# Long convolution by residues of four: value spectra and inverse over 256 bins, folds on VectorE, five of sixteen product rows on POOL

## The chip, the core and the metric

The kernel runs on one core of a Trainium2 chip. TensorE (PE; its weight loads are listed apart as PEld), VectorE (DVE), ScalarE (ACT), GpSimd (POOL) and SyncE (SP, which here only issues transfers) each run their own list of instructions in order and meet at semaphores. The metric is the device time of one execution of the whole program in microseconds, as a median over runs.

## What is computed

Two layers of a diffusion backbone over 1024 latent tokens and 256 context tokens of width 1024, all in f32. Layer 0 mixes by gated linear attention and by a long convolution over 512 channels; layer 1 by a short convolution; each is followed by a mixture of 32 experts. The change touches only the long convolution of layer 0:

```python
def hyena_filters(L, ...):          # filters h_fwd, h_bwd of length L = 1024, 512 channels each
    ...
    hh = (hh @ w3).reshape(L, 2, HY_WIDTH) * window[:, None]
    return hh[:, 0], hh[:, 1]

def bidir_fftconv(u, h_fwd, h_bwd, skip):
    L = u.shape[1]
    n = 2 * L
    U = jnp.fft.rfft(uf, n=n, axis=1)
    K = jnp.fft.rfft(h_fwd, n=n, axis=0) + jnp.conj(jnp.fft.rfft(h_bwd, n=n, axis=0))
    y = jnp.fft.irfft(U * K[None], n=n, axis=1)[:, :L]
    return y + uf * skip

def hyena_mix(p, filt, conv_w, conv_b, skip):
    x0, x1, v = jnp.split(dwconv3(p, conv_w, conv_b), 3, axis=-1)
    return x0 * bidir_fftconv(v * x1, filt[0], filt[1], skip)
```

## The kernel before, in words

Everything is f32 and lives in one SBUF tensor, `arena`, cut into named pieces by offset; pieces that are dead are given to others, and a semaphore orders the two uses. PSUM has eight banks of 128x512. The spectra are not computed by an FFT but by matmuls with tables of cosines and sines: time is split into even and odd tokens (`par`, 2), the 512 bins into four blocks of 128 (`kt`, 4), and there is a cosine and a sine table (`fn`, 2). The order of all work is the order in which each engine's list is written; there is no scheduler.

The stretch that the change touches runs, per engine, like this.

- **DVE, end of the attention heads.** `hyena_conv` forms `VX` = v * x1, channel block by channel block; the product is L2023 and raises `vx_ready`. The last of four comes at the end of `gla_head(3)`.
- **SP.** After the last projection (`hy_mm`) it loads the filters' hidden layer `HH2` (L593), the filter weights `W3H` (L594) and the 4 MB table `DFT` (L595), in this order. When the filters are windowed (`filt_win`) it loads the 4 MB inverse table `IDFT` (L598). Later it loads two halves of the output projection (L463) and, after the last inverse matmul (`idft_mm`), the 4 MB residual input (L606).
- **PE, `hyena_transposes` (L1379)** turns `VX` to time on partitions; ACT copies it to `VTM` (L976).
- **PE, `spectrum(kt, q)` (L1395).** For each bin block eight spectra of four matmuls 128x512 each, accumulated in one bank: q = 0 to 3 of the values `VTM`, q = 4 to 7 of the filters `HSUM`/`HDIF`. For kt = 0 the four value spectra come first, then the filters are made, then the rest follows.
- **Filters, eight steps t.** PE multiplies `HH2` by `W3H` into two banks (L1412), ACT copies one bank (L987), DVE forms sum and difference (L2041, L2042) and windows the sum (L2046), POOL windows the difference (L702). Between them PE and DVE spread a gate row (L1181, L1895).
- **Products.** ACT copies each spectrum out of PSUM into `UK` (L995), eight pieces of 128x512. There is one `UK`, so the copies of block kt wait until the products of block kt - 1 are done. The spectrum product of a block is four rows of `YF` (real and imaginary parts for even and odd tokens); a row is seven instructions, four products and three sums. DVE makes rows 0 and 2 (L2055, L2058, L2061, L2064), POOL rows 1 and 3 (L713, L717, L720, L725): eight rows each over the four blocks. On DVE, every instruction of a row but the second waits for the one ahead of it (`link`); on POOL each waits (`step`).
- **PE, inverse (L1437).** 4 channel blocks x 2 parities x 2 functions x 4 bin blocks = 64 matmuls 128x512. The first 48 need the products of blocks 0 to 2, the last 16 those of block 3.
- **DVE** adds the skip term and gates (L2073, L2076), `hmix_ready`; then PE starts the output projection (L1474), and DVE adds the residual (L2088, L2089), after the load L606.

## Time and profile before

| | us |
|---|---|
| median of 3 runs | 2678.17 |
| lowest and highest run | 2674.11, 2680.32 |
| the profiled execution | 2692.55 |
| its span (first to last instruction of the profile) | 2690.6 |

The profile is of one execution, which took 14.4 us more than the median. Times inside it are counted from the start of its span. The touched stretch lies between 549 and 751 us of the span. A profile row of the timeline reads: start in us, length in us, engine, line of the kernel, operation, output<-input, shapes, how many instructions were merged, and in square brackets how long the engine was idle before and what released it. One f32 matmul appears as two records on PE and two weight loads on PEld.

### The profile page before, as it was taken

The numbers are of one execution on the slowest core, as the hardware profiler recorded it, in microseconds if no ns is written. First come the engines' busy times: TensorE is split into PE (matmuls) and PEld (weight loads), VectorE is DVE, ScalarE is ACT, GpSimd is POOL, SyncE is SP. The second block draws the span as 40 slices with busy tenths as digits, with TensorE's granted clock in tenths as the row PEclk, the third lists the DMA queues.
The fourth block names the chain that finished last, engine by engine and source line by source line (L and its number), as shares of the span: only waits on it lengthen the run. The fifth ranks groups of instructions, "written<-read, shape, count | busy, mean of one in ns | idle before, by whom it ended". The sixth has DMA issues, their size and how long they took to land. (4 is left out here: it accounts for less than half of the span.)

```text
span 2690.6 us, 33060 instructions
## 1 busy us (share of the span) xinstructions
PE 2498.0 (93%) x14463; PEld 1114.3 (41%) x14464; DVE 1026.4 (38%) x1958; ACT 340.0 (13%) x664; POOL 242.9 (9%) x227
## 2 busy tenths in 40 slices
PE   5999989989999899999999799999999999999991
PEld 3455445544445533333333544444556333333330
DVE  2687477747656422222221411011464222222114
ACT  2211233321011100000000310000111000000001
POOL 2000000017600000000000000000000000000000
PEclk8999999989999899999999899999998999999995
DMA  9475001210120689999998611110006999999975
GB/s 335 173 261 196 16 24 32 77 79 10 63 86 29 255 341 388 381 392 379 371 370 348 222 39 41 30 55 31 24 32 259 355 390 392 398 398 385 382 281 216
DMA packets 121869, 574.15 MB, mean 213 GB/s; under 512 B 11743, under 2 KB 48807, under 8 KB 94712
## 3 DMA queue, kind: packets, MB, share of 16 engines
q1 hardware_dynamic: 104328, 528.56, 51.5%
q0 software_dynamic: 17312, 43.16, 4.1%
q8 instruction: 116, 1.90, 0.3%
q10 hardware_dynamic: 80, 0.26, 0.0%
q14 instruction: 33, 0.27, 0.0%
HBM read 550.71 MB, written 38.01 MB: 219 GB/s over the span
## 5 line engine op out<-in xcount | busy, mean ns | idle before, releaser
L1609 PE MATMUL ps<-arena 128*32 128x512 f32 x6144 | 689.7, 601 | 30.7 <-DMA arena<-in_ex_w_dram 30.3
L1609 PEld LDWEIGHTS ps<-arena 128*32 128x32 f32 x6144 | 199.0, 111 | 453.4 <-issue 452.2
L1633 PE MATMUL ps<-arena 128*32 128x512 f32 x3072 | 343.5, 599 | 12.2 <-DMA arena<-in_ex_w_dram 12.2
L1711 PE MATMUL ps<-arena 128*128 128x512 f32 x768 | 333.3, 596 | 4.5 <-ACT arena L1013 4.5
L2275 DVE TENSOR_SCALAR arena<-ps,gain_x,mod 128x128 f32<-128x128 f32 x384 | 126.8, 402 | 374.4 <-PE ps L1594 374.4
L1474 PE MATMUL ps<-arena 128*128 128x512 f32 x512 | 226.6, 597 | 2.9 <-DVE arena L2076 1.6
L1711 PEld LDWEIGHTS ps<-arena 128*128 128x128 f32 x768 | 146.7, 191 | 188.5 <-issue 188.5
L1633 PEld LDWEIGHTS ps<-arena 128*32 128x32 f32 x3072 | 108.0, 111 | 238.7 <-issue 238.7
L2307 DVE SCALAR_TENSOR_TENSOR arena<-ps,arena,gates 128x512 f32<-128x512 f32 x96 | 72.1, 751 | 268.1 <-PE ps L1633 268.1
L1294 PE MATMUL ps<-arena 128*128 128x512 f32 x384 | 167.3, 593 | 0.7 <-issue 0.7
L2283 DVE TENSOR_TENSOR arena<-arena,ps 128x512 f32<-128x512 f32 x48 | 52.5, 1094 | 273.5 <-PE ps L1609 273.5
L1474 PEld LDWEIGHTS ps<-arena 128*128 128x128 f32 x512 | 95.1, 190 | 113.3 <-issue 109.1
L1073 ACT ACTIVATE arena<-ps 128x512 f32<-128x512 f32 x48 | 28.7, 597 | 745.3 <-PE ps L1576 745.3
L2409 DVE TENSOR_TENSOR arena<-arena,ps 128x1024 f32<-128x1024 f32 x8 | 9.8, 1222 | 284.8 <-PE ps L1711 284.8
L1395 PE MATMUL ps<-arena 128*128 128x512 f32 x256 | 113.6, 607 | 3.8 <-DVE arena L2046 3.1
L744 POOL DMA_INDIRECT expert_rows<-arena x48 | 48.1, 1003 | 754.6 <-DVE arena L2307 754.6
L1294 PEld LDWEIGHTS ps<-arena 128*128 128x128 f32 x384 | 72.0, 190 | 88.1 <-issue 87.6
L1863 DVE SCALAR_TENSOR_TENSOR arena<-arena,silu_c 128x512 f32<-128x512 f32 x120 | 90.2, 752 | 4.3
L734 POOL DMA_INDIRECT arena<-normed_rows,arena x48 | 48.7, 1014 | 377.6 <-PE ps L1594 302.2
L1395 PEld LDWEIGHTS ps<-arena 128*128 128x128 f32 x256 | 49.7, 195 | 66.6 <-issue 61.7
L1071 ACT ACTIVATE arena<-ps 128x512 f32<-128x512 f32 x48 | 28.7, 598 | 355.1 <-PE ps L1609 355.1
L1125 PE MATMUL ps<-constants 128*128 128x256 f32 x270 | 72.1, 419 | 0.0
(276 smaller groups left out, 2193.3 us busy)
## 6 DMA issues: line engine op xcount, KB each, us to landing
arena<-in_ex_w_dram SPq DMA_DIRECT2D x192, 2048.0 KB, 11.9
arena<-in_mod_w_dram SPq DMA_DIRECT2D x24, 2048.0 KB, 8.7
arena<-expert_rows SPq DMA_DIRECT2D x16, 1024.0 KB, 8.1
arena<-in_od_w_in_dram SPq DMA_DIRECT2D x24, 512.0 KB, 6.4
arena<-in_x_dram SPq DMA_DIRECT2D x2, 4096.0 KB, 14.8
normed_rows<-arena POOLq DMA_DIRECT2D x16, 512.0 KB, 2.9
arena<-in_ev_w_in_dram SPq DMA_DIRECT2D x3, 2048.0 KB, 13.1
arena<-in_ev_w_in_dram SPq DMA_DIRECT2D x12, 512.0 KB, 4.2
```

Of the source, the lines that this page charges most:

```text
L734: pool.indirect_dma_start(XG[:, b], None, rows_hn, bass.IndirectOffsetOnAxis(ap=PASS_TOK[:, p:p + 1], axis=0), bounds_check=SEQ - 1, oob_i ...
L1125: nc.tensor.matmul(bank(b)[:, 0:256], ident, cst[:, 0:256], start=True, stop=True)
L1294: ins = nc.tensor.matmul(bank(6 + half), HYP[n % 3][:, j], u_part(half, j), start=j == 0, stop=j == KC - 1)
L1395: ins = nc.tensor.matmul(bank((q + 4) % 8), DFT[:, kt, fn, par, tc * P:(tc + 1) * P], rhs, start=tc == 0, stop=tc == KT - 1)
L1474: ins = nc.tensor.matmul(bank(m % 4), mixed[:, j, i * P:(i + 1) * P], slab(first[half], KC, 512)[:, j], start=j == 0, stop=j == KC - 1)
L1609: ins = nc.tensor.matmul(bank(2 + m)[c:c + n], x[:, j, c:c + n], w_slot(e % 2, m, KC, FE)[:, j], start=j == 0, stop=j == KC - 1)
L1633: ins = nc.tensor.matmul(bank(5 + half)[c:c + n], HT[:, j * P + c:j * P + c + n], w_slot(e % 2, 2, FC, D)[:, j, half * 512:(half + 1) * 51 ...
L1711: ins = nc.tensor.matmul(bank(2 * k + half), slab(L1_IN + c, 3, KC, P)[:, k, j], u_part(half, j), start=j == 0, stop=j == KC - 1)
L1863: link(V.scalar_tensor_tensor(out=acc, in0=w[:, j], scalar=silu_c[:, j, 0:1], in1=acc, op0=ALU.mult, op1=ALU.add))
L2275: ins = V.tensor_scalar(XT[:, b, j * P:(j + 1) * P], bank(j // 4)[:, (j % 4) * P:(j % 4 + 1) * P], gain_x[:, 2 * l + 1, j:j + 1], mod[:, l ...
L2283: return V.tensor_tensor(HS.rearrange("t (c p) -> t p c", p=P), SL.rearrange("t (p c) -> t p c", c=FC), bank(3).rearrange("t (p c) -> t p ...
L2307: V.scalar_tensor_tensor(out=YS[:, b, cs], in0=bank(5 + half), scalar=PASS_GATE[:, p:p + 1], in1=gates[:, 1, cs], op0=ALU.mult, op1=ALU.mu ...
```

## The change

The value sequence is now split by token number modulo four instead of two (`times(par, tc)` gives tokens `par + 2 * (tc // 2) + 4 * ...`). Bins k and 511 - k of a residue differ only in signs and in the swap of cosine and sine, so the spectra of the values are computed for 256 bins, two groups g of 128, and the other 256 follow by sums and differences.

- **`residue(g, i, s)`** replaces the value half of `spectrum`. For each group g and each (function, parity) i it accumulates two matmuls in each of two banks (s = 0, 1): 2 x 4 x 2 x 2 = 32 matmuls 128x512 in place of 64, all ahead of the filters. ACT copies the second bank to `USECOND`, DVE adds and subtracts it from the first bank into `USUM[g]` (16 instructions, semaphore `butterfly`). `USUM[1]` lies over `VTM`, so DVE starts the eight of group 1 when all 16 pairs of matmuls are done. PE starts the filters when six of these eight are done (the second step when all are).
- **`filter_spectrum(kt, q)`**: the 64 filter matmuls as before. They alternate between two sets of four banks, and ACT copies them into `KB`, which has two slots, so block kt waits for the products of kt - 2.
- **Products.** POOL makes rows 1 and 3 of block 0 and row 3 of the others: five rows. DVE makes the other eleven.
- **Folds.** After blocks 1 and 3 DVE folds the two blocks of a group: four sums or differences (`tensor_tensor`) and four `scalar_tensor_tensor` with the scalar -2 or 2, in place in `YF`, 16 instructions in all.
- **Inverse.** For each group, channel block and residue r two matmuls with 256 columns, written to every second column of a bank (`bank(2 * c + r % 2)[:, r // 2::2]`): 64 matmuls of 128x256 in place of 64 of 128x512. Group 0 starts after the first fold, group 1 after the second. `IDFT` is 2 MB in place of 4 MB.
- **Space.** `HH2` now lies over the buffer that DVE reads as x1 for the last `VX`. SP therefore waits for the last `vx_ready` before it loads `HH2`; `W3H` and `DFT` stand behind it in SP's list.

PE's list from the last transposes to the end of the inverse, before (L1379 transposes, L1395 spectra, L1412 filters, L1181 gate row, L1437 inverse):

```order
L1379 MATMUL ps<-constants,arena 128x128 x8
L1395 MATMUL ps<-arena 128x512 x16
L1412 MATMUL ps<-arena 128x512 x4
L1181 MATMUL ps<-constants,mod 128x64 x8
...
L1395 MATMUL ps<-arena 128x512 x112
L1437 MATMUL ps<-arena 128x512 x64
```

and now (L1420 residues, L1451 filters, L1430 filter spectra, L1474 inverse):

```order
L1403 MATMUL ps<-constants,arena 128x128 x8
L1420 MATMUL ps<-arena 128x512 x32
L1451 MATMUL ps<-arena 128x512 x4
L1205 MATMUL ps<-constants,mod 128x64 x8
...
L1430 MATMUL ps<-arena 128x512 x64
L1474 MATMUL ps<-arena 128x256 x64
```

Sixteen more matmuls stand ahead of the filters, 48 fewer behind them, and the inverse has the same count at half the columns.

SP's list around the table load, before:

```order
L593 DMA arena<-filter_hidden 64x1024 [waits flt_in,hy_mm]
L594 DMA arena<-in_hy_w_dram 64x1024
L595 DMA arena<-in_dft_dram 128x8192
L598 DMA arena<-in_idft_dram 128x8192 [waits filt_win]
```

and now:

```order
L617 DMA arena<-filter_hidden 64x1024 [waits vx_ready,flt_in,hy_mm]
L618 DMA arena<-in_hy_w_dram 64x1024
L619 DMA arena<-in_dft_dram 128x8192
L622 DMA arena<-in_idft_dram 128x4096 [waits filt_win]
```

The wait for `vx_ready` is new, and `DFT` is behind it.

DVE's list at the end of block 1, now (L2105 ends a product row, L2115 and L2118 are the fold, L2099 and L2102 begin the next block's first row); before, the next block's row followed at once:

```order
L2105 TENSOR_TENSOR arena<-arena 128x512 [waits dve_step]
L2115 TENSOR_TENSOR arena<-arena 128x512 [waits yf_pool,yf_dve]
L2115 TENSOR_TENSOR arena<-arena 128x512 x3
L2118 SCALAR_TENSOR_TENSOR arena<-arena 128x512 [waits butterfly] x4
L2099 TENSOR_TENSOR arena<-arena 128x512 [waits uk_ready,butterfly]
L2102 TENSOR_TENSOR arena<-arena 128x512
L2108 TENSOR_TENSOR arena<-arena 128x512 [waits dve_step]
```

Eight instructions of DVE have come in between two blocks, and again behind the last.

```diff
--- before.py
+++ after.py
@@ -91,18 +91,18 @@
+    low = np.arange(HALF // 2).reshape(2, P)
+    k = np.stack([low[0], HALF - 1 - low[0], low[1], HALF - 1 - low[1]]).reshape(HALF)
@@ -192,11 +192,33 @@
-        IDFT = at(38912, 2, 2, KT * HALF)
+        IDFT = at(38912, 2, 2, SEQ)
...
-        UK = at(0, 8, HW)
+        USUM = [at(0, 8, HW), at(34816, 8, HW)]
+        USECOND = at(30720, 4, HW)
+        KB = at(43008, 2, 4, HW)
+        POOL_ROWS = ((1, 3), (3,), (3,), (3,))
+        DVE_ROWS = [[r for r in range(4) if r not in rows] for rows in POOL_ROWS]
+        def rows_before(rows, kt):
+            return sum(len(r) for r in rows[:kt])
+        def times(par, tc):
+            first = par + 2 * (tc // 2) + 4 * (tc % 2) * P
+            return slice(first, first + 4 * P - 3, 4)
+        def product_terms(kt, row):
+            ua, ub, uc, ud = [USUM[kt // 2][:, 4 * (kt % 2) + q] for q in range(4)]
+            ka, kb, kc, kd = [KB[:, kt % 2, q] for q in range(4)]
+            return (((ua, ka), (ub, kb), (uc, kc), (ud, kd)),
+                    ((ua, kb), (ub, ka), (uc, kd), (ud, kc)),
+                    ((ua, kc), (ub, kd), (uc, ka), (ud, kb)),
+                    ((ua, kd), (ub, kc), (uc, kb), (ud, ka)))[row], ((1, -1, -1), (1, 1, 1))[row // 2]
+        def quarter(g, r, fn):
+            return YF[:, 2 * g + r // 2, (2 * fn + r % 2) if r < 3 else 3 - 2 * fn]
...
-        HH2_EARLY, HH2, W3H = at(47104, SEQ), at(2304, SEQ), at(21504, SEQ)
+        HH2_EARLY, HH2, W3H = at(47104, SEQ), at(20480, SEQ), at(21504, SEQ)
@@ -590,17 +613,18 @@
+            sp.wait_ge(vx_ready, HC)
@@ -704,26 +728,24 @@
-                pool.wait_ge(uk_ready, 8 * (kt + 1))
...
+                pool.wait_ge(butterfly, 8 * (kt // 2 + 1))
+                pool.wait_ge(uk_ready, 8 + 4 * (kt + 1))
...
+                for done, row_ in enumerate(POOL_ROWS[kt]):
+                    terms, signs = product_terms(kt, row_)
@@ -977,22 +999,24 @@
-            for q in range(4):
-                act.wait_ge(dft_mm, q + 1)
-                nc.scalar.activation(UK[:, q], bank((q + 4) % 8), ACT.Copy).then_inc(uk_ready, 1)
+            for g in range(2):
+                for i in range(4):
+                    act.wait_ge(dft_mm, 8 * g + 2 * i + 2)
+                    if g:
+                        act.wait_ge(butterfly, 2 * (i + 1))
+                    nc.scalar.activation(USECOND[:, i], bank((2 * i + 4) % 8 + 1), ACT.Copy).then_inc(uk_ready, 1)
...
-                if kt:
-                    act.wait_ge(yf_dve, 2 * kt)
-                    act.wait_ge(yf_pool, 2 * kt)
-                for q in range(0 if kt else 4, 8):
-                    act.wait_ge(dft_mm, 8 * kt + q + 1)
-                    nc.scalar.activation(UK[:, q], bank((q + 4) % 8), ACT.Copy).then_inc(uk_ready, 1)
+                if kt >= 2:
+                    act.wait_ge(yf_dve, rows_before(DVE_ROWS, kt - 1))
+                    act.wait_ge(yf_pool, rows_before(POOL_ROWS, kt - 1))
+                for q in range(4):
+                    act.wait_ge(dft_mm, 16 + 4 * kt + q + 1)
+                    nc.scalar.activation(KB[:, kt % 2, q], bank(4 * (kt % 2) + q), ACT.Copy).then_inc(uk_ready, 1)
@@ -1377,7 +1401,7 @@
-                                                  VX[:, c, par + 2 * tc * P:par + 2 * (tc + 1) * P - 1:2], ident)
+                                                  VX[:, c, times(par, tc)], ident)
@@ -1385,36 +1409,51 @@
-            def spectrum(kt, q):
-                fn, par = (q % 4) // 2, q % 2
-                if kt:
-                    pe.wait_ge(uk_ready, 8 * (kt - 1) + q + 1)
+            def residue(g, i, s):
+                fn, par = i % 2, i // 2
+                if g:
+                    pe.wait_ge(butterfly, 2 * (i + 1))
+                elif i == 2:
+                    pe.wait_ge(omix_ready, 2 * HEADS)
+                for tc in (2 * s, 2 * s + 1):
+                    ins = nc.tensor.matmul(bank((2 * i + 4) % 8 + s), DFT[:, 2 * g, fn, par, tc * P:(tc + 1) * P], VTM[:, par, tc],
+                                           start=tc == 2 * s, stop=tc == 2 * s + 1)
+                ins.then_inc(dft_mm, 1)
+            def filter_spectrum(kt, q):
+                fn, par = q // 2, q % 2
+                if kt >= 2:
+                    pe.wait_ge(uk_ready, 8 + 4 * (kt - 2) + q + 1)
...
-                    rhs = VTM[:, par, tc] if q < 4 else (HSUM, HDIF)[fn][:, par * KT + tc]
-                    ins = nc.tensor.matmul(bank((q + 4) % 8), DFT[:, kt, fn, par, tc * P:(tc + 1) * P], rhs,
-                                           start=tc == 0, stop=tc == KT - 1)
+                    ins = nc.tensor.matmul(bank(4 * (kt % 2) + q), DFT[:, kt, fn, par, tc * P:(tc + 1) * P],
+                                           (HSUM, HDIF)[fn][:, par * KT + tc], start=tc == 0, stop=tc == KT - 1)
...
-                for q in range(4):
-                    spectrum(0, q)
+                for g in range(2):
+                    for i in range(4):
+                        for s in range(2):
+                            residue(g, i, s)
...
+                    else:
+                        pe.wait_ge(butterfly, 14 + 2 * t)
...
-                                         HH2[0:HID, par + 2 * tc * P:par + 2 * (tc + 1) * P - 1:2],
+                                         HH2[0:HID, times(par, tc)],
...
-                            pe.wait_ge(uk_ready, 4)
+                            pe.wait_ge(butterfly, 16)
@@ -1422,38 +1461,32 @@
-                    for q in range(8):
-                        if kt == 1 and q == 0:
-                            pe.wait_ge(mod_gate, 4)
-                        if kt or q >= 4:
-                            spectrum(kt, q)
+                    if kt == 1:
+                        pe.wait_ge(mod_gate, 4)
+                    for q in range(4):
+                        filter_spectrum(kt, q)
...
-                def part(c, par, kts, first, last):
+                def part(c, r, g):
...
-                        for kt in kts:
-                            ins = nc.tensor.matmul(
-                                bank(2 * (c % 4) + par), YF[:, kt, 2 * fn + par, c * P:(c + 1) * P],
-                                IDFT[:, fn, par, kt * HALF:(kt + 1) * HALF],
-                                start=first and fn == 0 and kt == kts[0], stop=last and fn == 1 and kt == kts[-1])
+                        ins = nc.tensor.matmul(
+                            bank(2 * c + r % 2)[:, r // 2::2], quarter(g, r, fn)[:, c * P:(c + 1) * P],
+                            IDFT[:, g, fn, r * 256:(r + 1) * 256],
+                            start=g == 0 and r < 2 and fn == 0, stop=g == 1 and r >= 2 and fn == 1)
...
-                pe.wait_ge(yf_dve, 2 * (KT - 1))
-                pe.wait_ge(yf_pool, 2 * (KT - 1))
-                for c in range(HC):
-                    for par in range(2):
-                        q = (2 * c + par + 4) % 8
-                        pe.wait_ge(uk_ready, 8 * (KT - 1) + q + 1)
-                        part(c, par, list(range(KT - 1)), True, False)
-                pe.wait_ge(yf_dve, 2 * KT)
-                pe.wait_ge(yf_pool, 2 * KT)
-                for c in range(HC):
-                    for par in range(2):
-                        part(c, par, [KT - 1], False, True).then_inc(idft_mm, 1)
+                for g in range(2):
+                    pe.wait_ge(butterfly, 16 + 8 * (g + 1))
+                    for c in range(HC):
+                        for par in range(2):
+                            if g == 0:
+                                pe.wait_ge(uk_ready, 16 + 2 * c + par + 1)
+                            part(c, par, g)
+                            ins = part(c, par + 2, g)
+                            if g:
+                                ins.then_inc(idft_mm, 1)
@@ -2032,6 +2065,17 @@
+            for g in range(2):
+                u = USUM[g]
+                for i, (plus, minus, turned) in enumerate(((0, 4, 0), (2, 6, 1), (1, 7, 0), (3, 5, 0))):
+                    dve.wait_ge(dft_mm, 16 if g else 2 * (i + 1))
+                    dve.wait_ge(uk_ready, 4 * g + i + 1)
+                    first, second = bank((2 * i + 4) % 8), USECOND[:, i]
+                    V.tensor_tensor(u[:, plus], first, second, ALU.add).then_inc(butterfly, 1)
+                    if turned:
+                        first, second = second, first
+                    V.tensor_tensor(u[:, minus], first, second, ALU.subtract).then_inc(butterfly, 1)
@@ -2047,11 +2091,11 @@
-                dve.wait_ge(uk_ready, 8 * (kt + 1))
...
+                dve.wait_ge(butterfly, 8 * (kt // 2 + 1))
+                dve.wait_ge(uk_ready, 8 + 4 * (kt + 1))
...
+                for done, row_ in enumerate(DVE_ROWS[kt]):
+                    terms, signs = product_terms(kt, row_)
@@ -2059,9 +2103,20 @@
+                if kt % 2:
+                    g = kt // 2
+                    dve.wait_ge(yf_pool, rows_before(POOL_ROWS, kt + 1))
+                    y, z = YF[:, kt - 1], YF[:, kt]
+                    folds = ((y[:, 0], z[:, 0], 1), (y[:, 2], z[:, 2], -1), (y[:, 1], z[:, 3], 1), (y[:, 3], z[:, 1], 1))
+                    for p, q, sign in folds:
+                        V.tensor_tensor(p, p, q, ALU.add if sign > 0 else ALU.subtract).then_inc(butterfly, 1)
+                    for n, (p, q, sign) in enumerate(folds):
+                        dve.wait_ge(butterfly, 16 + 8 * g + n + 1)
+                        V.scalar_tensor_tensor(out=q, in0=q, scalar=-2.0 * sign, in1=p, op0=ALU.mult, op1=ALU.add)\
+                            .then_inc(butterfly, 1)
```

## Rows read from the trace of the kernel before

**Rows 1.** The page, first part: busy time of each engine, share, instructions.

```profile
PE 2498.0 (93%) x14463; PEld 1114.3 (41%) x14464; DVE 1026.4 (38%) x1958; ACT 340.0 (13%) x664; POOL 242.9 (9%) x227
```

**Rows 2.** Busy time by stretch: start:end, length, each engine, granted clock, DMA share, GB/s.

```profile
core 0: us, PE busy (x) PEld busy (x) DVE busy (x) ACT busy (x) POOL busy (x), PEclk, DMA share, GB/s
552.27:567.60 15.33, 15.33 (x32) 6.58 (x32) 0.00 (x0) 1.79 (x3) 0.00 (x0) 0.91 0.00 0
567.60:595.90 28.30, 24.28 (x97) 14.71 (x96) 24.51 (x28) 5.37 (x9) 10.62 (x8) 0.88 0.00 1
595.90:612.36 16.46, 16.46 (x34) 7.25 (x35) 0.55 (x2) 2.39 (x4) 0.00 (x0) 0.89 0.63 256
612.36:636.00 23.64, 23.64 (x57) 10.46 (x56) 22.05 (x14) 0.01 (x1) 22.49 (x14) 1.00 0.00 0
636.00:718.20 82.20, 82.03 (x192) 36.20 (x191) 66.18 (x42) 12.07 (x24) 66.48 (x42) 1.00 0.08 26
718.20:749.45 31.25, 31.23 (x73) 13.49 (x71) 10.08 (x14) 0.00 (x0) 1.04 (x1) 1.00 0.20 68
```

**Rows 3.** Timeline and DMA list (KB each, us to landing): the tables and the first spectra.

```profile
528.51 0.49 SPq L593 DMA_DIRECT2D arena<-filter_hidden  x1
529.69 0.58 SPq L595 DMA_DIRECT2D arena<-in_dft_dram  x1
...
arena<-in_dft_dram SPq DMA_DIRECT2D x1, 4096.0 KB, 14.6
arena<-in_idft_dram SPq DMA_DIRECT2D x1, 4096.0 KB, 12.6
...
548.32 1.22 DVE L2023 TENSOR_TENSOR arena<-arena 128x1024 f32<-128x1024 f32 x1
...
552.27 15.42 PE L1395 MATMUL ps<-arena 128*128 128x512 f32 x32 [0.69 <-ACT arena L976]
```

**Rows 4.** Timeline: DVE in a filter step, and PE's restart behind the filters.

```profile
570.33 0.69 DVE L2041 TENSOR_TENSOR arena<-ps,arena 128x512 f32<-128x512 f32 x1 [19.46 <-issue]
570.93 0.68 DVE L2042 TENSOR_TENSOR arena<-ps,arena 128x512 f32<-128x512 f32 x1
...
595.90 4.63 PE L1395 MATMUL ps<-arena 128*128 128x512 f32 x6 [3.08 <-DVE arena L2046]
```

**Rows 5.** Timeline: products on DVE and POOL, and ACT's copies behind them.

```profile
612.36 0.69 DVE L2055 TENSOR_TENSOR arena<-arena 128x512 f32<-128x512 f32 x1 [15.91 <-ACT arena L995]
...
614.25 1.59 POOL L717 TENSOR_TENSOR arena<-arena 128x512 f32<-128x512 f32 x1
...
614.75 1.64 DVE L2064 TENSOR_TENSOR arena<-arena 128x512 f32<-128x512 f32 x1
...
616.43 1.64 DVE L2058 TENSOR_TENSOR arena<-arena 128x512 f32<-128x512 f32 x1
...
635.99 4.03 ACT L995 ACTIVATE arena<-ps 128x512 f32<-128x512 f32 x8 [23.67 <-POOL arena L720]
...
640.13 0.69 DVE L2055 TENSOR_TENSOR arena<-arena 128x512 f32<-128x512 f32 x1 [5.34 <-ACT arena L995]
```

**Rows 6.** Timeline: DVE and POOL instructions of 512 columns with the other engine silent.

```profile
549.46 1.40 DVE L2000 SCALAR_TENSOR_TENSOR arena<-ps,cols,arena 128x512 f32<-128x512 f32 x2
...
577.40 1.26 POOL L702 TENSOR_TENSOR arena<-arena 128x512 f32<-128x512 f32 x1 [2.42 <-DVE arena L2042]
...
762.46 0.69 DVE L2088 TENSOR_TENSOR arena<-ps,gates 128x512 f32<-128x512 f32 x1 [11.52 <-DMA arena<-in_x_dram]
763.19 0.69 DVE L2089 TENSOR_TENSOR arena<-arena 128x512 f32<-128x512 f32 x1
```

**Rows 7.** Timeline: matmuls of 256 columns, of 64 spread columns, and the inverse.

```profile
220.93 3.70 PE L1257 MATMUL ps<-arena 128*128 128x256 f32 x16
...
571.25 2.00 PE L1181 MATMUL ps<-constants,mod 128*128 128x64 f32 x16
...
694.26 55.17 PE L1437 MATMUL ps<-arena 128*128 128x512 f32 x128 [0.17 <-ACT arena L995]
```

More of the change, by code:

```diff
@@ L329, in build @@
         uk_ready = sem("uk_ready")
+        butterfly = sem("butterfly")
         yf_dve = sem("yf_dve")
@@ L705, in _ @@
             for kt in range(KT):
-                pool.wait_ge(uk_ready, 8 * (kt + 1))
-                ua, ub, uc, ud, ka, kb, kc, kd = [UK[:, q] for q in range(8)]
+                pool.wait_ge(butterfly, 8 * (kt // 2 + 1))
+                pool.wait_ge(uk_ready, 8 + 4 * (kt + 1))
                 t0, t1 = CTMP[:, 2], CTMP[:, 3]
-                for row_, terms, signs in ((1, ((ua, kb), (ub, ka), (uc, kd), (ud, kc)), (1, -1, -1)),
-                                           (3, ((ua, kd), (ub, kc), (uc, kb), (ud, ka)), (1, 1, 1))):
+                for done, row_ in enumerate(POOL_ROWS[kt]):
+                    terms, signs = product_terms(kt, row_)
                     base += 1
@@ L717, in _ @@
                         step(nc.gpsimd.tensor_tensor(t1, x, y, ALU.mult), base)
-                        dst = YF[:, kt, row_] if q == 2 else t0
+                        op = ALU.add if signs[q] > 0 else ALU.subtract
                         if q == 2:
-                            nc.gpsimd.tensor_tensor(
-                                dst, t0, t1, ALU.add if signs[q] > 0 else ALU.subtract).then_inc(yf_pool, 1)
-                            pool.wait_ge(yf_pool, 2 * kt + row_ // 2 + 1)
+                            nc.gpsimd.tensor_tensor(YF[:, kt, row_], t0, t1, op).then_inc(yf_pool, 1)
+                            pool.wait_ge(yf_pool, rows_before(POOL_ROWS, kt) + done + 1)
                         else:
                             base += 1
-                            step(nc.gpsimd.tensor_tensor(
-                                dst, t0, t1, ALU.add if signs[q] > 0 else ALU.subtract), base)
+                            step(nc.gpsimd.tensor_tensor(t0, t0, t1, op), base)
             def gather(l, p):
@@ L2049, in _ @@
             for kt in range(KT):
-                dve.wait_ge(uk_ready, 8 * (kt + 1))
-                ua, ub, uc, ud, ka, kb, kc, kd = [UK[:, q] for q in range(8)]
+                dve.wait_ge(butterfly, 8 * (kt // 2 + 1))
+                dve.wait_ge(uk_ready, 8 + 4 * (kt + 1))
                 t0, t1 = CTMP[:, 0], CTMP[:, 1]
-                for row_, terms, signs in ((0, ((ua, ka), (ub, kb), (uc, kc), (ud, kd)), (1, -1, -1)),
-                                           (2, ((ua, kc), (ub, kd), (uc, ka), (ud, kb)), (1, 1, 1))):
+                for done, row_ in enumerate(DVE_ROWS[kt]):
+                    terms, signs = product_terms(kt, row_)
                     step(V.tensor_tensor(t0, terms[0][0], terms[0][1], ALU.mult))
```

18 lines of the change are left out of this document (8 added, 10 removed).

## Prediction

> **What bounds the kernel now.** I read the page's first part, then busy time by stretch, then the timeline of each engine across the touched part. PE is busy 93% of the span and DVE 38% [rows 1], so less work on PE looks like a gain; the question is whether PE ends last in this stretch and still would. By stretch [rows 2]: from 552.27 the 16 value matmuls of block 0 (15.33 us), from 567.60 the filters (28.30, in which PE, ACT and DVE hand each step on in turn), from 595.90 the filter matmuls of block 0 until the first product (16.46), then 105.84 us from 612.36 to 718.20 in which PE is full (82.03 of 82.20) and DVE and POOL nearly so (66.18 and 66.48 of 82.20; 22.05 and 22.49 of 23.64 in block 0). Last, 31.25 us of inverse alone. Two things stand close together here: PE, and the pair DVE with POOL. An engine at 66 of 82 is no cover for much more work.
>
> Why DVE and POOL are so full: a DVE product lasts 0.69 us at the start of a block and 1.64 while POOL works, with starts 1.68 apart (614.75, 616.43), and POOL's lasts 1.59 [rows 5]. With the other silent, DVE starts the next linked instruction after 0.73 us (762.46, 763.19) and POOL needs 1.26 [rows 6]. Each POOL instruction thus costs DVE 1.68 - 0.73 = 0.95 us; they do not run side by side.
>
> That agrees with the Trainium skill, "SBUF — State Buffer", section "Who interferes with whom": a DVE instruction with two SBUF inputs and a GpSimd one that reads SBUF exclude each other for the whole instruction. By that rule, taken with whole durations, my sum below would be 2697.5; the trace agrees with the exclusion, not with its full length, and I go by the row.
>
> **The change step by step**, in times of the profiled execution.
>
> (a) The table. SP issued L593 at 528.51 and `DFT` 1.18 later, which landed 14.6 after its issue; the last `vx_ready` comes at 548.32 + 1.22 = 549.54 [rows 3]. Now SP waits for it with `HH2`, and `W3H` and `DFT` are queued behind. `DFT` is there at 549.54 + 1.18 + 14.6 = 565.3, and PE, which started at 552.27, waits for it: **+13.0**. The other 4 MB table landed in 12.6 [rows 3]: bound +11.0. Nothing hides this; PE's next work all needs the table. The strided transposes lie in this wait and cost nothing.
>
> (b) 16 more value matmuls ahead of the filters. 64 matmuls took 55.17 us, 0.86 each [rows 7]: **+13.8**. Their butterflies and copies for group 0 run beside PE (DVE idle 19.46 us there, [rows 4]), and banks are free a group later.
>
> (c) The eight butterflies of group 1 start only after the last matmul, and the filters wait for six. Unlinked instructions on DVE start 0.60 apart (570.33, 570.93) [rows 4]: 3.6, and 0.2 for the semaphores: **+3.8**.
>
> (d) PE then restarts after a pause. What that costs is seen at 595.90, after 3.08 us idle [rows 4]: the stretch took 16.46 at a mean granted clock of 0.89 [rows 2], so partly at the lower level of 1.2 GHz, where 16 matmuls are 13.8, one ACT copy 0.5 (4.03 / 8, [rows 5]) and semaphores 0.2. So 1.9 are lost, and as the first filter steps pass through PE in turn: **+1.9** (bounds 0 and 1.9).
>
> Filter matmuls then start 13.0 + 13.8 + 3.8 + 1.9 = 32.5 later, at 628.4, and the first product (16.46 unchanged) at 644.9. The 48 value matmuls that are gone behind this point were PE's; PE now needs 64 x 0.86 = 55 us for the filters and is done at about 685, long before the products.
>
> (e) DVE. Eleven rows of seven; alone a row is 0.60 + 6 x 0.73 = 5.0: 55.0. The folds: four unlinked at 0.60 and four `scalar_tensor_tensor` at 0.70 (two in 1.40, [rows 6]), 5.2, twice: 10.4. POOL's five rows are 35 instructions, all of them while DVE is busy: 35 x 0.95 = 33.3. Together **98.7** against 105.84: **-7.1**, end at 743.6. The gaps of about 4 to 5 us between blocks (5.34, [rows 5]) go, since `KB` has two slots: block 2's copies run while block 1 is multiplied. POOL pauses before block 3 until DVE ends block 1, which moves its instructions but not their number. Bounds: linked instructions at 0.60 in the 36 places where DVE is alone, -4.7; pairs as long as the two lone durations together, 1.26 + 0.69 = 1.95, +9.5. I take 1.68, since the rows show it with the same two kinds of instruction.
>
> (f) Inverse. Group 0 starts near 705 and is hidden behind the products. Group 1, 32 matmuls of 256 columns, stands bare: 16 records of 256 columns took 3.70 with the last one's tail [rows 7], so half of 0.86 holds, 13.8; PE has been idle some 20 us, so the restart again, 1.9: **15.7** against 31.25: **-15.6**. Writing to every second column is not in the trace; nearest are 16 records of 64 columns to every eighth in 2.00, 0.125 each [rows 7], which shows no penalty but could hide a doubling: bounds 0 and +13.8. I take 0.
>
> (g) Hidden: the second half of the output weights is issued at about 738 and, half of a 14.6 us table, is there by 753 for a use near 766. `IDFT` is half as long and 80 us early. The residual load L606 follows the last inverse matmul as before, and DVE waits for it as before (11.52, [rows 6]), so the end moves with the inverse.
>
> **Sum**: 32.5 - 7.1 - 15.6 = **+9.8**. The profiled execution would go from 2692.55 to 2702.4; on the median, 2678.17, this is **2688.0**. PE loses 32 + 32 matmuls' worth (55 us) and the path gains none of it: behind the filters 22.7 are won, ahead of them 32.5 are lost.
>
> **Rivals.**
>
> *Slow inverse.* The half-wide matmuls do not run at half the time. The Trainium skill ("TensorE: Matmul & The Clock Gate", section "The mechanism") says that a weight load overlaps with matmuls in flight only when they sit in different row groups, which full 128-row matmuls never do. A load is 36.20 / 191 = 0.19 us [rows 2]; laid bare in group 1, 64 x 0.19 = 12.2: **2700.2**. Against it: 16 records of 256 columns with 16 such loads in 3.70, where bare loads would make 6.5 [rows 7]. Doubled writes would give +13.8: 2701.8. Together 0.08.
>
> *Small prices all low.* DVE starts linked instructions 0.60 apart (-4.7) and PE restarts at no cost (-3.8): +1.3, **2679.5**, no difference. For it: both are bounds read off rows; against it, the pairs with a link at 0.73 [rows 6] and the 0.89 clock [rows 2]. 0.12.
>
> *Faster.* DVE and POOL stop excluding each other, because their operands now lie elsewhere in `arena` (`USUM`, `KB` in place of one `UK`). DVE then takes 0.73 throughout, 33.3 less, while POOL alone needs 35 x 1.26 = 44 and does not bind: 9.8 - 33.3 = -23.5, **2654.7**. It breaks even at a pair of 1.68 - 9.8 / 35 = 1.40 us and is faster by more than 0.2% below 1.24. Against it: 1.64 and 1.59 in every block, whatever the operands (66.18 and 66.48 us for 42 instructions each, [rows 2]). 0.04.
>
> **How the numbers follow.** Forecast 0.76, between about +4 (table in 12.6, one restart free, part of the link bound) and +19 (pairs at 1.95): 2682 to 2697.5. The range takes in most of the no-difference rival too: 2678 to 2698. What a measurement of this kernel can tell from no change is about 0.2%, 5.4 us. Slower: 0.73 of the forecast and the slow inverse, 0.81. Same: 0.03 and 0.11, 0.14. Faster: 0.05.
>
> **What the profile after would show.** (a) PE's first value matmul at 565, released by the DMA of `DFT`, not by ACT. (b, c) last value matmul near 594, first filter matmul 4 us later, released by DVE. (e) DVE without a gap from 645 to 743, with 1.64 us instructions as long as POOL runs and 0.69 behind it; POOL with one pause of some 7 us. (f) PE idle from about 685 to 705 and 721 to 743, then 32 matmuls in 15.7. The prediction is wrong if the table lands with PE not waiting, if DVE's pairs are not 1.68, or if the last 32 matmuls take over 20 us.

## The result and the profile after

| | before | after |
|---|---|---|
| median, us | 2678.17 (5 runs) | 2701.21 (5 runs) |
| lowest and highest | 2671.59, 2680.32 | 2695.31, 2706.11 |
| span of the profiled execution | 2690.6 | 2704.1 |

The ratio is 1.0077, with a 95% interval of 1.0059 to 1.0095: the change makes the kernel slower by 23.0 us on the medians. The direction was as forecast; the forecast was +9.8.

The page of the changed kernel begins so (busy time, share of the span, instructions; [rows 1] answers to it):

```profile
span 2704.1 us, 32967 instructions
PE 2466.2 (91%) x14399; PEld 1116.0 (41%) x14400; DVE 1045.4 (39%) x2011; ACT 336.7 (12%) x656; POOL 208.5 (8%) x206
```

PE is busy for 31.8 us less than in [rows 1], and the whole takes longer. Busy time by stretch, with the boundaries at the steps of the prediction, answers to [rows 2]:

```profile
core 0: us, PE busy (x) PEld busy (x) DVE busy (x) ACT busy (x) POOL busy (x), PEclk, DMA share, GB/s
562.38:592.30 29.92, 29.92 (x64) 12.93 (x64) 5.15 (x8) 4.18 (x7) 0.00 (x0) 0.92 0.00 1
596.19:638.33 42.14, 41.85 (x96) 24.05 (x97) 26.20 (x30) 4.78 (x8) 10.60 (x8) 0.52 0.00 0
638.33:654.87 16.54, 16.54 (x35) 7.31 (x36) 0.55 (x1) 2.39 (x4) 0.00 (x0) 0.89 0.36 128
654.87:753.54 98.67, 56.76 (x159) 31.39 (x157) 96.36 (x93) 6.62 (x12) 55.75 (x35) 0.82 0.10 34
753.54:769.90 16.36, 16.29 (x64) 13.68 (x64) 10.11 (x15) 0.00 (x0) 0.00 (x0) 0.86 0.13 50
```

The second row is the surprise. It is the filters, and PE has the same matmuls in it as before (96 records, 97 in [rows 2]), but is busy for 41.85 us of 42.14 where it was busy for 24.28 of 28.30, at a mean granted clock of 0.52: the lower level, 1.2 GHz, for nearly the whole stretch. The other rows are close to what was forecast. The timeline of PE (start, length, line, operation; in brackets the idle time before and what ended it):

```profile
562.38 29.95 PE L1420 MATMUL ps<-arena 128*128 128x512 f32 x64 [12.77 <-DMA arena<-in_dft_dram]
596.19 6.00 PE L1451 MATMUL ps<-arena 64*128 64x512 f32 x8 [3.87 <-DVE arena L2077]
602.12 3.67 PE L1205 MATMUL ps<-constants,mod 128*128 128x64 f32 x16
605.73 7.21 PE L1451 MATMUL ps<-arena 64*128 64x512 f32 x8
...
638.33 57.00 PE L1430 MATMUL ps<-arena 128*128 128x512 f32 x128 [0.29 <-DVE arena L2090]
...
753.54 16.29 PE L1474 MATMUL ps<-arena 128*128 128x256 f32 x64 [21.31 <-DVE arena L2118]
```

The wait for the table, the wait for the butterflies and the inverse of 256 columns are all where they were expected. What was not: a pair of filter steps (four matmuls with 64 rows of weights, eight records) takes 7.21 us, and a gate row 3.67. In the timeline of the kernel before, the same lists take 3.71 and, as in [rows 7], 2.00:

```profile
573.18 3.71 PE L1412 MATMUL ps<-arena 64*128 64x512 f32 x8
```

By steps, each from the end of the last `VX` product (549.54 before, 547.58 after) to the end of the inverse:

| step | before | after | measured | forecast |
|---|---|---|---|---|
| (a) `VX` to first value matmul | 2.73 | 14.80 | +12.1 | +13.0 |
| (b) value matmuls | 15.33 | 29.94 | +14.6 | +13.8 |
| (c) pause for butterflies | 0 | 3.87 | +3.9 | +3.8 |
| (d) filters | 28.30 | 42.14 | **+13.8** | +1.9 |
| until the first product | 16.46 | 16.54 | +0.1 | 0 |
| (e) products and folds | 105.84 | 98.67 | -7.2 | -7.1 |
| (f) inverse, bare part | 31.23 | 16.29 | -14.9 | -15.6 |
| sum | 199.89 | 222.25 | **+22.4** | +9.8 |

The sum agrees with the medians (+23.0), and 11.9 of the 12.6 us that the forecast lacks are step (d). The two spans differ by 13.5 us only, since everything outside these steps took 8.9 us less in the profile after. What stands behind the inverse took between 1919 and 1941 us in the profiles of this case (1941.2 before, 1934.3 after). I take that for the scatter of single executions, and from here on the kernels are compared over the stretch from the start of the last transposes to the end of the inverse: 199.8 us before, 222.2 after.

### The profile page after: what moved, and what is told of

Its sections match the earlier page's. It is cut to its first block and busy times, and to the rows that moved or that the text cites. A ratio compares the mean times of both kernels' runs of the same rounds, so it can differ in the third digit from the quotient of the medians.

```text
span 2704.1 us, 32967 instructions
## 1 busy us (share of the span) xinstructions
PE 2466.2 (91%) x14399; PEld 1116.0 (41%) x14400; DVE 1045.4 (39%) x2011; ACT 336.7 (12%) x656; POOL 208.5 (8%) x206
## 5 line engine op out<-in xcount | busy, mean ns | idle before, releaser
L1744 PE MATMUL ps<-arena 128*128 128x512 f32 x768 | 334.9, 599 | 4.5 <-ACT arena L1037 3.1
L1507 PE MATMUL ps<-arena 128*128 128x512 f32 x512 | 226.6, 597 | 2.9 <-DVE arena L2131 1.6
L1744 PEld LDWEIGHTS ps<-arena 128*128 128x128 f32 x768 | 147.7, 193 | 189.1 <-issue 189.1
L1318 PE MATMUL ps<-arena 128*128 128x512 f32 x384 | 167.3, 594 | 0.7 <-issue 0.7
L1507 PEld LDWEIGHTS ps<-arena 128*128 128x128 f32 x512 | 95.4, 191 | 112.6 <-issue 108.8
L1318 PEld LDWEIGHTS ps<-arena 128*128 128x128 f32 x384 | 72.2, 191 | 87.9 <-issue 87.4
L1242 PE MATMUL ps<-arena 128*128 128x512 f32 x160 | 71.2, 602 | 0.0
L1474 PE MATMUL ps<-arena 128*128 128x256 f32 x128 | 32.6, 423 | 41.9 <-DVE arena L2118 21.3
```

Source lines behind the costliest of these rows:

```text
L1242: ins = nc.tensor.matmul(bank((2, 3, 6)[i % 3]), u_cols(i, j), w[:, j], start=j == 0, stop=j == KC - 1)
L1318: ins = nc.tensor.matmul(bank(6 + half), HYP[n % 3][:, j], u_part(half, j), start=j == 0, stop=j == KC - 1)
L1507: ins = nc.tensor.matmul(bank(m % 4), mixed[:, j, i * P:(i + 1) * P], slab(first[half], KC, 512)[:, j], start=j == 0, stop=j == KC - 1)
L1744: ins = nc.tensor.matmul(bank(2 * k + half), slab(L1_IN + c, 3, KC, P)[:, k, j], u_part(half, j), start=j == 0, stop=j == KC - 1)
```

## Experiments on the filters: why the clock was low

My theory after the result: PE stands still for 3.87 us, its clock drops to the lower level, and the filter matmuls with their gate rows do not bring it back, so that PE runs 42 us of work at 1.2 GHz. The first two windows of the filters show where it fell:

```profile
596.19:602.12 5.93, 5.93 (x8) 2.46 (x8) 3.03 (x5) 0.60 (x1) 1.15 (x1) 0.62 0.00 0
602.12:605.70 3.58, 3.58 (x17) 3.49 (x16) 2.71 (x3) 0.60 (x1) 1.88 (x2) 0.50 0.01 2
```

A mean of 0.62 over 5.93 us is about 1.4 us at the full level and the rest at half (an estimate from this row): here the clock fell only when PE was at work again. In the execution with the table first, below, the first pair takes 7.18 us and is slow from its start. The pause comes before the fall in both. Rivals: the 12.77 us wait for the table ahead of the values did it, or the new way of reading `HH2` (tokens modulo four, a stride of four in the weights) makes these matmuls slow.

**The pause filled.** Nine matmuls of 256 columns with the identity, whose result nobody reads, run while DVE makes the butterflies:

```diff
                             residue(g, i, s)
+                pe.wait_ge(uk_ready, 5)
+                spare(9, 5)
                 pe.wait_ge(flt_in, 96)
```

> The changed kernel with nine idle matmuls of 256 columns (into a bank that nobody reads any more) between the last value matmul and the filters, so that PE does not stand still while DVE forms the eight butterflies of group 1; they are work on no result. Theory (clock): the pause of 3.87 us is what put PE to 1.2 GHz for the whole filter stretch, so the stretch from the first filter matmul to the first filter spectrum goes from 42.1 us back to about 28.5, and the time falls by about 13.6 us against the changed kernel, to a ratio near 1.003 of the kernel before. Rival (stride): the filters are slower since HH2 is read at every fourth token instead of every second; then the stretch stays at 42 us and the ratio at 1.008. Rival (long wait): the 12.8 us wait for the table is what the clock does not recover from; then it also stays at 42.

Measured: ratio 1.0019 (0.9999 to 1.0039), stretch 208.7, that is 13.5 less than the changed kernel. PE's timeline and the window of the filters:

```profile
592.61 4.05 PE L1149 MATMUL ps<-constants 128*128 128x256 f32 x18
596.64 3.79 PE L1453 MATMUL ps<-arena 64*128 64x512 f32 x8
600.36 2.00 PE L1205 MATMUL ps<-constants,mod 128*128 128x64 f32 x16
596.64:625.03 28.39, 24.53 (x98) 18.15 (x97) 25.58 (x30) 4.78 (x8) 10.62 (x8) 0.89 0.00 1
```

The same filter matmuls, with the same stride, on the same data, take 28.39 us at 0.89. The wait on `uk_ready` only makes sure that the bank (5, the second number of `spare`) has been copied out. The fill ends when the butterflies end and costs nothing. This already speaks against the stride. Filling the pause does not keep the clock up to the end: the last gate row of this run takes 3.39 us, behind a wait of 0.66 us inside the steps.

**The table first.** The changed kernel's load of `DFT` ahead of the wait for `VX`, back where nothing holds it:

```diff
             sp.wait_ge(flt_in, 64)
+            sp.dma_start(at(12288, 8192), a["dft"]).then_inc(tables_in, 16)
             sp.wait_ge(vx_ready, HC)
...
             sp.dma_start(W3H[0:HID], a["hy_w3"][0]).then_inc(flt_in, 16)
-            sp.dma_start(at(12288, 8192), a["dft"]).then_inc(tables_in, 16)
```

> The changed kernel with the DFT table's load put ahead of SP's wait for the last vx_ready, so that only HH2 and W3H stand behind that wait. Theory: the 12.8 us that PE waits for the table vanish (first value matmul about 2.7 us after the last transposes, released by ACT), the filter stretch stays at 42.1 us since the pause ahead of it is unchanged, and the time falls by about 12 us against the changed kernel, ratio near 1.0035. Rival (long wait): if the long wait is what leaves PE at 1.2 GHz in the filters, the filter stretch falls to 28 us too and the time by 26 us, ratio near 0.998. Rival (hidden): something else holds PE at this place, HH2 or W3H landing late; then the gain is under 5 us.

Measured: 1.0014 (0.9994 to 1.0035), stretch 211.8 (-10.4). Timeline and filter window:

```profile
552.12 30.73 PE L1420 MATMUL ps<-arena 128*128 128x512 f32 x64 [0.69 <-ACT arena L998]
586.72:630.04 43.32, 43.03 (x97) 24.09 (x97) 26.20 (x30) 4.78 (x8) 10.60 (x8) 0.50 0.00 0
```

The 12.77 us wait is gone (0.69), and the filters still take 43.32 us at 0.50. The stretch gains 10.4 us and not 12.1, since the value matmuls took 0.8 us and the filters 1.2 us longer in this execution. The long wait did not cause the low clock; the short pause right ahead of the filters did.

**The kernel before with the table late.** The reverse, alone: the wait for `VX` ahead of the three loads in the kernel before.

```diff
             sp.wait_ge(flt_in, 64)
+            sp.wait_ge(vx_ready, HC)
             sp.dma_start(HH2[0:HID], filter_hidden).then_inc(flt_in, 16)
```

> The kernel before with one line of the change alone: SP waits for the last vx_ready ahead of HH2, W3H and DFT. Theory: PE waits about 12 us for the table, the filters follow the value matmuls without a pause and keep 28.3 us, and the time rises by 12 to 13 us, ratio near 1.0047. Rival (long wait): after such a wait the filters run at 1.2 GHz; then +26 us, ratio near 1.0097.

Measured: 1.0036 (1.0023 to 1.005), stretch 213.35, which is 13.5 more than before. Timeline and filter window:

```profile
565.68 15.77 PE L1396 MATMUL ps<-arena 128*128 128x512 f32 x32 [13.66 <-DMA arena<-in_dft_dram]
...
581.38:609.67 28.29, 23.92 (x98) 14.37 (x97) 24.51 (x28) 5.37 (x9) 10.61 (x8) 0.89 0.00 1
```

Step (a) by itself costs about what the forecast gave it (13.0), and a wait of 13.66 us, followed by value matmuls without a pause behind them, leaves the filters at 28.29 us.

**The stride.** `HH2` read with a stride of two in place of four, all else as in the changed kernel:

```diff
-                                         HH2[0:HID, times(par, tc)],
+                                         HH2[0:HID, par + 2 * tc * P:par + 2 * (tc + 1) * P - 1:2],
```

> The changed kernel with HH2 read at every second token as in the kernel before; the filters' tokens are then in an order that does not fit the rest, so the convolution is another one, with the same amount of work. Theory (clock): nothing moves, the filter stretch stays at 42.1 us with a granted clock near one half. Rival (stride): it falls to 28 us.

Measured, one profiled execution of 2696.6 us: stretch 222.1, filters

```profile
597.48:639.39 41.91, 41.62 (x96) 23.44 (x97) 26.20 (x30) 4.78 (x8) 10.60 (x8) 0.52 0.00 0
```

as in the changed kernel. The stride rival falls.

**Fill in the middle of the filters.** The pause is left as it is, and nine of the same 256-column matmuls stand behind the first pair of steps. If it is the kind of matmul that decides, the clock comes back there; if the filters would have stayed low whatever comes between, it does not.

```diff
                             pe.wait_ge(butterfly, 16)
+                            pe.wait_ge(uk_ready, 8)
+                            spare(9, 7)
                         gate_part(0, t // 4, t // 2 % 2)
```

> The changed kernel with the nine idle matmuls not in the pause but behind it, after the second filter step, where PE is already at 1.2 GHz and busy without a gap. Theory A (what the work is): full 128x128 by 256 matmuls bring the clock back where the filters' 64-row matmuls and the gate row's 64-column ones do not; the filter stretch is then about 37 us in place of 42.1, in spite of the added work. Theory B (nothing inside the stretch brings it back): the fillers run at half rate too and the stretch becomes 42.1 + 7.7 = 49.8 us.

One profiled execution, 2695.7 us; the filters, fill included, take 38.08 us. Timeline of the fill, and three windows in order of time:

```profile
603.96 6.66 PE L1149 MATMUL ps<-constants 128*128 128x256 f32 x18
596.85:604.00 7.15, 7.15 (x9) 2.52 (x9) 3.03 (x5) 0.60 (x1) 1.19 (x1) 0.50 0.00 0
604.00:610.40 6.40, 6.40 (x19) 5.26 (x19) 3.04 (x3) 0.60 (x1) 1.84 (x2) 0.60 0.01 1
610.40:634.93 24.53, 19.37 (x90) 14.41 (x88) 19.77 (x22) 3.58 (x6) 7.58 (x6) 0.96 0.00 1
```

PE is busy without a gap in the first window (7.15 of 7.15) and stays at 0.50. During the fill, of matmuls with all 128 rows and 256 columns, the clock returns, and the rest of the filters runs at 0.96. So a busy PE was not enough here: behind the pause the filter matmuls with 64 rows and the gate rows of 64 columns ran at 0.50 for 40 us, and with nine matmuls of 128 rows and 256 columns between them the clock came back. Which of the two, the rows or the columns, makes the difference was not tried apart, and this is one execution.

Nor do the filters hold the full level once they have it. At the end of the same steps in the kernel before, PE waits for 0.94 us, and the gate row that follows takes 3.62 us in place of 2.00:

```profile
584.35 1.99 PE L1412 MATMUL ps<-arena 64*128 64x512 f32 x4
587.29 1.99 PE L1412 MATMUL ps<-arena 64*128 64x512 f32 x4 [0.94 <-DVEq L2045]
589.21 3.62 PE L1181 MATMUL ps<-constants,mod 128*128 128x64 f32 x16
```

The clock is thus already low there, ahead of the 3.08 us pause of [rows 4].

## Experiments on the products: the exchange between DVE and POOL

**POOL makes no row, on the changed kernel.** All sixteen rows on DVE.

```diff
-        POOL_ROWS = ((1, 3), (3,), (3,), (3,))
+        POOL_ROWS = ((), (), (), ())
```

> The changed kernel with all sixteen product rows on DVE and none on POOL. Theory (exclusion): each POOL instruction costs DVE 0.95 us and a DVE instruction alone costs 0.73, so the stretch from the first product to the last inverse group goes from 98.7 to 16 x 5.0 + 10 = 90 us, 8.7 less, though DVE does 35 instructions more; ratio near 1.0045. Rival (offload): POOL's share is work taken off DVE; without it the stretch grows by about 35 x 0.73 = 25 us, ratio near 1.017.

Measured: 1.0045 (1.0027 to 1.0063), stretch 214.3 (-7.9; the table was 1.4 us later in this execution), products and folds:

```profile
656.35:745.48 89.13, 56.20 (x159) 30.88 (x157) 85.80 (x128) 6.73 (x12) 0.00 (x0) 0.85 0.11 38
```

DVE makes 35 more instructions and ends 9.5 us earlier.

**POOL makes eight rows**, two in each block.

```diff
-        POOL_ROWS = ((1, 3), (3,), (3,), (3,))
+        POOL_ROWS = ((1, 3), (1, 3), (1, 3), (1, 3))
```

> The changed kernel with eight rows on POOL and eight on DVE, as in the kernel before. Exclusion: 8 x 5.0 + 10.4 + 56 x 0.95 = 103.6 us from the first product to the last inverse group, 5 more than with five rows. Offload: fewer than 98.7 us, near 84.

One profiled execution, 2717.0 us, stretch 229.2:

```profile
656.47:761.08 104.61, 56.77 (x159) 31.32 (x158) 101.71 (x72) 6.62 (x12) 89.03 (x56) 0.80 0.09 33
```

With 0, 35 and 56 instructions on POOL the stretch takes 89.13, 98.67 and 104.61 us: 0.27 us more for each that goes to POOL up to 35, 0.28 from there to 56. The prediction's two prices give 0.95 - 0.73 = 0.22 for an instruction given to POOL: it costs DVE more to be shut out than to do the work. The run with eight rows is a single execution. In one place of the changed kernel both prices stand side by side. DVE's and POOL's timeline, from where POOL pauses:

```profile
699.10 1.63 DVE L2105 TENSOR_TENSOR arena<-arena 128x512 f32<-128x512 f32 x1
...
702.32 0.68 DVE L2102 TENSOR_TENSOR arena<-arena 128x512 f32<-128x512 f32 x1
703.03 0.69 DVE L2108 TENSOR_TENSOR arena<-arena 128x512 f32<-128x512 f32 x1
...
700.26 1.59 POOL L744 TENSOR_TENSOR arena<-arena 128x512 f32<-128x512 f32 x1
708.89 1.39 POOL L737 TENSOR_TENSOR arena<-arena 128x512 f32<-128x512 f32 x1 [7.05 <-ACT arena L1019]
```

DVE takes 1.63 while POOL works and 0.69 as soon as it is silent.

**POOL makes no row, on the kernel before.** Rows 1 and 3 go to DVE's list; POOL's own loop of them and the waits for it leave the program:

```diff
                 for row_, terms, signs in ((0, ((ua, ka), (ub, kb), (uc, kc), (ud, kd)), (1, -1, -1)),
-                                           (2, ((ua, kc), (ub, kd), (uc, ka), (ud, kb)), (1, 1, 1))):
+                                           (1, ((ua, kb), (ub, ka), (uc, kd), (ud, kc)), (1, -1, -1)),
+                                           (2, ((ua, kc), (ub, kd), (uc, ka), (ud, kb)), (1, 1, 1)),
+                                           (3, ((ua, kd), (ub, kc), (uc, kb), (ud, ka)), (1, 1, 1))):
```

> The kernel before with all sixteen product rows on DVE and none on POOL, otherwise unchanged. Theory (PE ends last there): DVE needs 4 x 5.0 = 20 us for a block in place of 23.6, but PE needs 27.5 for its 32 matmuls and stays busy without a gap, so the time does not change, ratio 0.999 to 1.001, although the same edit took 9 us off the changed kernel. Rival: the products bound the kernel before as well; then it falls by 4 x 3.6 = 14 us, ratio near 0.9945.

Measured: 0.999 (0.9974 to 1.0006), stretch 199.5 (-0.4): no difference. Timeline of PE and, twice, DVE's first product of a block:

```profile
596.22 98.20 PE L1369 MATMUL ps<-arena 128*128 128x512 f32 x224 [3.11 <-DVE arena L2018]
...
640.23 0.69 DVE L2029 TENSOR_TENSOR arena<-arena 128x512 f32<-128x512 f32 x1 [7.74 <-ACT arena L969]
...
667.69 0.69 DVE L2029 TENSOR_TENSOR arena<-arena 128x512 f32<-128x512 f32 x1 [7.66 <-ACT arena L969]
```

The same edit that takes 9.5 us off the changed kernel takes nothing off this one. PE runs 98 us without a gap, and DVE, now faster, waits nearly 8 us for each block. Before, PE set the pace of the products with DVE close behind it; after, DVE alone sets it. That is why so little of the saved work on PE arrives: behind the filters 55 us of matmuls are gone, and the path there gets 22.1 us shorter (7.2 in the products, 14.9 in the inverse), since DVE ends next. Ahead of the first product the 16 value matmuls that moved there (+14.6), the two waits (+12.1 and +3.9) and the slow filters (+13.8) more than take it back.

## Two versions that beat both kernels

**Three edits together** (table first, pause filled, POOL without rows): the diffs are those shown.

> The changed kernel with three edits together: the DFT table loaded ahead of the wait for vx_ready, nine idle matmuls in the pause ahead of the filters, and all product rows on DVE. If the three parts add up, the stretch loses 12 + 13.5 + 8.7 = 34 us against the changed kernel and ends about 11.5 us earlier than in the kernel before: ratio near 0.9957. If the products without POOL then wait for something else (the copies into KB, or PE), the gain is 3 to 9 us smaller and the ratio 0.998 to 0.999.

Measured: **0.9932** (0.9909 to 0.9956), median 2663.6 us; stretch 187.9, which is 34.3 under the changed kernel and 11.9 under the kernel before. Alone the three gave 13.5 + 10.4 + 7.9 = 31.8. The 2.5 more are the later table in the run without POOL (1.4) and the longer filters in the run with the table first (1.2): they add up. The filters, the wait for the first product, the products:

```profile
586.20:614.59 28.39, 24.06 (x98) 17.68 (x97) 25.58 (x30) 4.78 (x8) 10.62 (x8) 0.90 0.00 1
614.59:631.55 16.96, 16.96 (x35) 7.44 (x36) 0.54 (x1) 2.39 (x4) 0.00 (x0) 0.87 0.34 124
631.55:720.69 89.14, 56.20 (x159) 30.88 (x158) 85.80 (x128) 6.73 (x12) 0.00 (x0) 0.83 0.11 38
```

The ratio is 18.2 us on 2680.35 (11.8 to 24.4), and the stretch accounts for 11.9. Where the other 6 lie is open. In every run with an interval the ratio gives 2 to 8 us less than the stretch; with the table first it gives +3.8 (-1.6 to +9.4) where the stretch says +12.0. So the stretch shows what each edit does in its place, and for the whole kernel the ratios stand.

**The pause behind the filters filled too.** The 0.87 in the second row is the restart of [rows 4], and as there the clock had fallen in the last filter step (its gate row takes 2.92 us); three spare matmuls inside the last steps and seven behind them:

```diff
                         gate_part(0, t // 4, t // 2 % 2)
+                        if t == 5:
+                            spare(3, 7)
...
             def transform():
+                pe.wait_ge(filt_ready, 7)
+                spare(7, 0)
                 pe.wait_ge(filt_win, 4 * KT)
```

> The kernel with the three edits together (table first, nine idle matmuls ahead of the filters, no product rows on POOL), and ten idle matmuls more: three after the sixth filter step and seven behind the last, while PE waits for the last windowed filter. Theory (clock): in the version with three edits PE falls to 1.2 GHz in the last filter step and restarts there; kept busy, the 16 filter matmuls of block 0 need 14.6 us until the first product instead of 16.9, and the stretch is 1 to 2 us shorter. Rival: the idle matmuls run over the end of the wait and cost what they give; then no change within 1 us. The ratio is near 0.993 to 0.995 either way.

Measured: **0.9929** (0.9906 to 0.9953), median 2662.9 us, stretch 184.8. Timeline of PE and of DVE's first product:

```profile
609.76 3.24 PE L1149 MATMUL ps<-constants 128*128 128x256 f32 x14
614.22 55.20 PE L1430 MATMUL ps<-arena 128*128 128x512 f32 x128 [1.22 <-DVE arena L2096]
628.97 0.69 DVE L2105 TENSOR_TENSOR arena<-arena 128x512 f32<-128x512 f32 x1 [14.20 <-ACT arena L1019]
```

From 614.22 to 628.97 are 14.75 us in place of 16.96: the low clock ahead of the first product was worth 2.2. The rest of the 3.1 us by which the stretch is shorter is in no row that the ten matmuls touch (the value matmuls took 29.40 in place of 30.72 and the last inverse group 16.59 in place of 16.15). In the median this is lost in the scatter; of the two, it is the better by the stretch alone.

## Why the prediction was right in direction and wrong in size

**(a) The table: right.** It landed 13.4 us after its issue, forecast 14.6; the late table in the kernel before cost 13.5.

**(b), (c): right.** +14.6 and +3.9 against +13.8 and +3.8. The value matmuls run at 0.92, against 0.91 in [rows 2].

**(d) PE's restart: the step that failed.** "So 1.9 are lost", with bounds 0 and 1.9. The row it came from, the restart at 595.90 in [rows 4], was misread twice. The clock had fallen ahead of that pause already, inside the filters (the gate row of 3.62 us at 589.21), so the row does not show what a pause of 3 us does. And it has matmuls of 128 rows and 512 columns behind it, with which the clock came back. Behind the new pause stand the filter matmuls and gate rows instead, and it stayed at the lower level for nearly all of their 42.14 us (mean 0.52). I also argued that the steps pass through PE in turn, and never asked what PE needs at half the clock. [rows 2] holds it: 24.28 us of PE work at a mean clock of 0.88 is 24.28 x 0.88 / 0.50 = 42.7 us at the lower level, an estimate (the mean takes in the idle time), and more than the 28.30 of the chain. The run with the table first, with 0.50 throughout, took 43.32. The upper bound of this step was thus +14.4 by the row, +15.0 by that run, and not +1.9, and the low clock turned PE from one of three engines that pass work on into the one that ends last. With the measured +13.8 in place of 1.9 my own sum is +21.7.

**(e) Products and folds: right to 0.1 us**, 98.67 against 98.7, by the pair at 1.68 and the lone price of 0.73. The gaps between blocks are gone as forecast, and POOL's one pause was 7.05 us. The stretches measured with 0 and 8 rows on POOL confirm the mechanism, with the slope a little steeper (0.27 in place of 0.22). That the sum is right to 0.1 is partly luck: by the same prices it is 90.4 with no row on POOL (measured 89.13) and 103.6 with eight (104.61), so it is 1.3 too high at one end and 1.0 too low at the other, and crosses the measured line near five rows. What I did not draw from my own prices is their consequence: if each POOL instruction costs DVE 0.95 and DVE's own costs 0.73, no row should go to POOL as soon as DVE ends last.

**(f) Inverse: right**, 16.29 against 15.7. My sentence that the path gains none of PE's saved 55 us was wrong by my own sum: the 22.7 us won behind the filters are just that gain, as far as DVE lets it through.

**(g) Hidden: right.** No wait for `IDFT` appears ahead of the last inverse group, which starts when DVE has made its last fold (L2118), and none for the output weights behind it: the output projection waits 1.57 us for DVE, as before.

**Rivals.** *Slow inverse* fell: the bare group is 64 records in 16.29 us, with 13.68 us of weight loads beside it in the same window. Bare loads would have made 15.7 + 12.2 = 27.9. The rule that I weighed there, of the Trainium skill ("TensorE: Matmul & The Clock Gate", section "The mechanism"), that full 128-row matmuls never overlap with their weight loads, does not hold in this trace. The same section also names a background weight buffer whose loads are pulled ahead; the trace would agree with that, but cannot show it. Nor did writing to every second column cost anything that shows in these 16.29 us. *Small prices all low* fell with the clock, which moved the other way. *Faster* fell: DVE and POOL exclude each other with the new operands as with the old, 1.63 and 1.59. By the section "Who interferes with whom" of the Trainium skill ("SBUF — State Buffer") they should, and the trace agrees; taken with whole durations, as there, the pair would be 1.95, and it is 1.67.

The range of 2678 to 2698 missed 2701.2 by 3 us, for one reason: the bound of (d) was taken from a row that had other work behind its pause.

## What to carry to other kernels

The price of a pause on PE need not be the pause and a fixed restart: ask which matmuls follow, take as the upper bound all the work at half the clock up to matmuls of a kind behind which a row of your trace shows the clock back, and if that is more than the chain around it, try to fill the pause with matmuls that nobody reads. Here each product instruction given to POOL cost DVE 0.95 us and saved it 0.73, so it is worth giving away only as long as DVE does not end last. Before a wait goes ahead of a load in SP's list, look at what is queued behind it. Relieving the engine that ends last (here PE, by 55 us) gains only until the next one does (here DVE, after 22.1).

## What the runs showed of the hardware that I had not expected

- PE was busy for 41.85 of 42.14 us at a mean granted clock of 0.52, after a pause of 3.87 us. The same list without the pause had 0.89 (28.39 us).
- Matmuls with 64 rows of weights and 512 columns, alternating with 128-row matmuls of 64 columns, left the clock at 0.50; nine 128-row matmuls of 256 columns raised it (0.60 over them, 0.96 behind).
- In the kernel before the clock fell inside the filters, where PE had waited for no more than 0.94 us: a gate row took 3.62 us in place of 2.00. With the pause ahead of the filters filled, it fell behind a wait of 0.66 us (3.39 us).
- Taking 35 instructions from POOL and giving them to DVE made the stretch shorter by 9.5 us.
- A wait of 13.66 us, followed by 16 matmuls of 128 rows and 512 columns, left no trace in the clock of the filters behind them (0.89).
